# Chunk loop of a state-space scan with its outputs made with features on partitions, and a last norm in another order, on one Trainium2 core

## The reference, cut to what matters

```python
cs = jnp.cumsum(da, axis=2)                      # da = dt * a, per token and head
lmat = jnp.exp(jnp.where(tril, seg, -jnp.inf))   # seg = cs[t] - cs[s]
cb = jnp.einsum('bctgn,bcsgn->bctsg', cc, bc)
y_diag = jnp.einsum('bctsg,bctsgr,bcsgrp->bctgrp', cb, lmat, xs)        # xs = x * dt
chunk_states = jnp.einsum('bctgn,bctgr,bctgrp->bcgrpn', bc, decay_to_end, xs)
y_off = jnp.einsum('bctgn,bcgrpn,bctgr->bctgrp', cc, h_prev, jnp.exp(cs))
y = (y_diag + y_off)
...
y = y + d_skip[:, None] * xh
...
x = rmsnorm(x, norm_final)
```

## Time and profile before

| | |
|---|---|
| median of 3 runs | 1798.56 us (1798.55 to 1800.17) |
| the profiled execution | 1797.06 us, of which the span from the first to the last instruction is 1795.3 us |
| TensorE busy (PE) | 1782.7 us, 99% of the span |
| VectorE (DVE), ScalarE (ACT), GpSimd (POOL) | 935.5, 637.8, 831.1 us |
| mean granted clock of TensorE | 0.996 |
| chunk loop | from 206.2 to about 293 us |
| last norm and stores | from about 1780.9 us to the end |

### The profile page before, as it was taken

The page is one execution under the profiler, slowest core; times in us unless marked ns, Lnnn a source line. Parts: engine busy times, 40 slices in busy tenths (PEclk is TensorE's granted clock), DMA queues, the critical chain, the costliest instruction groups (busy, mean ns, idle before and its releaser), DMA issues.

```text
span 1795.3 us, 34076 instructions
## 1 busy us (share of the span) xinstructions
PE 1782.7 (99%) x13933; PEld 1741.7 (97%) x13933; DVE 935.5 (52%) x1507; ACT 637.8 (36%) x986; POOL 831.1 (46%) x410
## 2 busy tenths in 40 slices
PE   9999999999999999999999999999999999999998
PEld 8999899999999999999999999999999999999997
DVE  6577785666515524556444441554655425515465
ACT  6436464443212312344433331333433212312343
POOL 4333313675544544566433333333465535444563
PEclk9999999999999999999999999999999999999999
DMA  6222231223232232232222222122222222222231
GB/s 239 81 87 73 94 110 68 82 83 111 102 130 93 83 101 86 68 112 83 86 80 80 68 75 91 71 80 80 69 83 94 82 94 82 98 90 85 62 102 51
DMA packets 59684, 161.04 MB, mean 90 GB/s; under 512 B 6960, under 2 KB 21296, under 8 KB 59584
## 3 DMA queue, kind: packets, MB, share of 16 engines
q1 hardware_dynamic: 53088, 151.03, 24.3%
q10 hardware_dynamic: 6496, 8.61, 1.5%
HBM read 153.94 MB, written 5.67 MB: 89 GB/s over the span
## 4 chain that ended last, share of the span: by engine, by line
PE 97%; DVE 1%; DMA 0%; ACT 0%; POOL 0%; issue 0%; ACTq 0%; DVEq 0%; POOLq 0%
PE proj L321 86%; PE Q L1063 6%; PE proj L1063 2%; DMA x<-in_x 0%; PE Q L1295 0%; PE Q L1373 0%; DVE arena L1969 0%; PE Q L1247 0%; PE Q L1329 0%; POOL arena L671 0%; DVE rstd L372 0%; PE Q L1321 0%; PE Q L1090 0%; PE Q L1330 0%; PE Q L333 0%
## 5 line engine op out<-in xcount | busy, mean ns | idle before, releaser
L417 POOL TENSOR_TENSOR w_lo<-w_raw,w_hi 128x1024 fp32r<-128x1024 f32 (+2 forms) x275 | 659.1, 2397 | 753.7 <-ACT w_hi L343 743.5
L321 PE MATMUL proj<-op_hi,w_hi 128*128 128x256 f32 x4208 | 880.1, 290 | 1.0 <-DVE op_lo L1564 0.4
L321 PE MATMUL proj<-op_hi,w_lo 128*128 128x256 f32 x4208 | 870.1, 288 | 0.0
L321 PE MATMUL proj<-op_lo,w_hi 128*128 128x256 f32 x4208 | 863.0, 286 | 0.0
L321 PEld LDWEIGHTS proj<-op_hi,w_hi 128*128 128x128 f32 x4208 | 672.7, 188 | 14.7 <-issue 11.4
L321 PEld LDWEIGHTS proj<-op_lo,w_hi 128*128 128x128 f32 x4208 | 675.2, 188 | 0.0
L321 PEld LDWEIGHTS proj<-op_hi,w_lo 128*128 128x128 f32 x4208 | 671.2, 188 | 0.0
L343 ACT ACTIVATE w_hi<-w_raw 128x1024 fp32r<-128x1024 f32 (+2 forms) x275 | 283.7, 1031 | 657.7 <-PE proj L321 652.6
L1634 DVE TENSOR_TENSOR arena<-proj,rstd 128x512 f32<-128x512 f32 x141 | 97.4, 691 | 209.0 <-PE proj L321 200.9
L1641 DVE TENSOR_TENSOR x<-proj,x 128x512 f32<-128x512 f32 x72 | 49.7, 690 | 240.9 <-PE proj L321 240.9
L678 ACT ACTIVATE arena<-arena 128x128 f32<-128x128 f32 (+6 forms) x298 | 129.1, 474 | 57.8 <-DVE arena L1637 29.8
(11 more groups left out here) (198 smaller groups left out, 1004.5 us busy)
## 6 DMA issues: line engine op xcount, KB each, us to landing
w_raw<-in_w_gu SPq DMA_DIRECT2D x88, 512.0 KB, 3.3
w_raw<-in_w_down SPq DMA_DIRECT2D x32, 512.0 KB, 3.2
w_raw<-in_w_heads_a SPq DMA_DIRECT2D x30, 512.0 KB, 3.3
w_raw<-in_w_heads_b SPq DMA_DIRECT2D x18, 512.0 KB, 3.2
w_raw<-in_w_gate SPq DMA_DIRECT2D x16, 512.0 KB, 3.3
w_raw<-in_w_xbc SPq DMA_DIRECT2D x12, 512.0 KB, 3.3
w_raw<-in_w_down SPq DMA_DIRECT2D x16, 384.0 KB, 2.9
w_raw<-in_w_u SPq DMA_DIRECT2D x8, 512.0 KB, 3.3
```

Source lines behind the costliest of these rows:

```text
L321: last = nc.tensor.matmul(proj[:, 2 * g.mod(2) + half, 0:size], w[:, lo:lo + P], o[:, at:at + size], start=(k == 0 and j == 0), stop=(k == ...
L417: nc.gpsimd.tensor_tensor(w_lo[:, c:c + width], w_raw[:, c:c + width], w_hi[:, c:c + width], ALU.subtract).then_inc(w_lo_done, 1)
```

## The change: what it does

The y turn is gone. `diagonal` takes `xs` as the stationary side (64 columns wide) and 128 columns of `mix` as the moving one, and writes even heads to partitions 0 to 63 and odd heads to 64 to 127 of PSUM. `from_state` takes four tiles of the state as stationary and C as moving, four products of 128 columns where there was one of 512. The outputs then stand with features on partitions. exp(cs) must now lie along the free axis: ScalarE makes it on the turned `cs_t`, it goes to DRAM (`ecs_rows`), and SyncE fetches it for each chunk but chunk 1 into `y_run`, spread over the partitions (`decays_in`, two DMAs). `off_scaled` waits for it. `xs` is made by VectorE straight from PSUM in two halves, so ScalarE's two copies of x are gone. At the end one `keep_warm` is gone, `spread(0)` comes after all sums, and the store of tile 3 moves from SyncE's queue to ScalarE's, ahead of the stores of tiles 0 to 2.

```diff
+            def decays_in(p):
+                c, rows = (NC, TS) if p == 0 else (p - 1, CH)
+                if p:
+                    sp.wait_ge(sem("y_stored"), 2 * p)
+                else:
+                    sp.wait_ge(sem("ecs_kept"), 16)
+                    sp.wait_ge(sem("x_silu"), XBC)
+                for odd in range(2):
+                    dst = y_run[odd * SP_:(odd + 1) * SP_, :].rearrange("p (f t) -> p f t", f=KD)[:, :, 0:rows]
+                    src = ecs_rows.rearrange("(f two) t -> two f t", two=2)[odd, :, c * CH:c * CH + rows]
+                    sp.dma_start(dst, src.unsqueeze(0).broadcast_to([SP_, KD, rows])).then_inc(sem("decays_in"), 16)
+
             for b in range(4):
                 rows_in(0, b)
             weights("outa")
             weights("z", only=0)
+            decays_in(0)
             for p in range(NC + 1):
                 if p < NC:
                     for b in range(4):
                         rows_in(p + 1, b)
                 for n in SSD_MIXED[p] + SSD_END[p]:
                     weights("z", only=n)
+                if FRESH <= p < NC:
+                    decays_in(p + 1)
...
                 for half in range(2):
                     if p:
-                        pe.wait_ge(sem("y_stored"), 2 * p - 1 + half)
+                        if p == FRESH + 1:
+                            pe.wait_ge(sem("y_stored"), 2 * p - 1 + half)
+                        else:
+                            pe.wait_ge(sem("y_sum"), (2 * p - 2 if p <= FRESH else 2 * p - 4) + half + 1)
...
                 def from_state(g):
-                    mm(Q[0:rows, 2 + g, :], cols(10 + g), state[:, g * 512:(g + 1) * 512]).then_inc(sem("y_off"), 1)
+                    for f in range(4):
+                        last = mm(Q[:, 2 + g, f * P:f * P + rows], state[:, (4 * g + f) * P:(4 * g + f + 1) * P], cols(10 + g))
+                    last.then_inc(sem("y_off"), 1)
...
                     for j in range(4):
                         h = 4 * b + j
-                        last = mm(Q[0:rows, b // 2, (h % 8) * SP_:(h % 8 + 1) * SP_],
-                                  mix[0:rows, b * 512 + j * P:b * 512 + j * P + rows], xs[0:rows, h * SP_:(h + 1) * SP_])
+                        odd, at = h % 2 * SP_, h % 8 // 2 * P
+                        last = mm(Q[odd:odd + SP_, b // 2, at:at + rows], xs[0:rows, h * SP_:(h + 1) * SP_],
+                                  mix[0:rows, b * 512 + j * P:b * 512 + j * P + rows])
...
-                for half in range(2):
-                    pe.wait_ge(sem("y_sum"), 2 * p + half + 1)
-                    for f in range(4):
-                        last = nc.tensor.transpose(Q[:, half, f * P:f * P + rows],
...
-                    last.then_inc(sem("y_turned"), 1)
...
-                    dve.wait_ge(sem("xs_done"), p + 1)
-                    tt(heads3(x_tok[:, g * 512:(g + 1) * 512]), Q[0:rows, 2 + g, :].rearrange("p (h q) -> p h q", q=SP_),
-                       per_head(ecs, 8 * g, 8, rows), mul).then_inc(sem("y_scaled"), 1)
+                    dve.wait_ge(sem("decays_in"), 32 * (p + 1 if p < FRESH else p))
+                    y = four(y_run[:, g * 512:(g + 1) * 512])[:, :, 0:rows]
+                    tt(y, four(Q[:, 2 + g, :])[:, :, 0:rows], y, mul).then_inc(sem("y_scaled"), 1)
...
                 token_sums(half, chunks, ssq, 0)
-                if half:
-                    keep_warm()
-                    spread(0, HALVES[0][2])
                 pe.wait_ge(sem("last_sq"), half + 1)
...
-            spread(1, HALVES[1][2])
+            for half, (at, size, chunks) in enumerate(HALVES):
+                spread(half, chunks)
```

More of the change, by code:

```diff
@@ L219, in build @@
         r = Region(temps)
-        x_tok, xs, xsd, mix = (r.take(n) for n in (D, D, D, 4 * 512))
+        y_run, xs, xsd, mix = (r.take(n) for n in (D, D, D, 4 * 512))
         z_buf = arena[:, temps:temps + 2 * T]
         s_prompt, s_sample = r.take(D), r.take(D)
-        (dt_b, da, cs, ecs, dte, etot, p_d) = (r.take(NP_) for _ in range(7))
+        (dt_b, da, cs, dte, etot, p_d) = (r.take(NP_) for _ in range(6))
         cs_t = v_sq[0:SH, 0:T]
+        ecs_t = v_sq[0:SH, VT:VT + T]
         cs_rows = nc.dram_tensor("cs_rows", (SH, T), F, kind="Internal").ap()
+        ecs_rows = nc.dram_tensor("ecs_rows", (SH, T), F, kind="Internal").ap()
         ms_v = ssq[:, 0:(NC + 1) * GROUPS]
@@ L567, in _ @@
             for half, (lo, size, chunks) in enumerate(HALVES):
-                for k in range(Y_POOL, KD):
+                for k in range(Y_POOL + 1, KD):
                     sp.wait_ge(sem("y_out"), half * (KD - Y_POOL) + k - Y_POOL + 1)
@@ L774, in _ @@
                     act.wait_ge(sem("cs_copied"), 1)
-                    run(ecs, cs, ACT.Exp)
+                    act.wait_ge(sem("cs_turned"), 2)
+                    run(ecs_t, cs_t, ACT.Exp, "ecs_turned")
+                    act.wait_ge(sem("ecs_turned"), 1)
+                    act.dma_start(ecs_rows, ecs_t).then_inc(sem("ecs_kept"), 16)
                     run(dte, dte, ACT.Exp)
@@ L1053, in _ @@
             for half, (lo, size, chunks) in enumerate(HALVES):
-                for k in range(Y_POOL):
-                    act.wait_ge(sem("y_pool"), half * Y_POOL + k + 1)
+                for k in (Y_POOL, *range(Y_POOL)):
+                    if k == Y_POOL:
+                        act.wait_ge(sem("y_out"), half * (KD - Y_POOL) + 1)
+                    else:
+                        act.wait_ge(sem("y_pool"), half * Y_POOL + k + 1)
                     act.dma_start(part(O["y"], k, lo, size), part(p_proj, k, lo, size)).then_inc(stored, 16)
@@ L1844, in chunk @@
                     .broadcast_to([rows, nh, SP_])
-                dve.wait_ge(sem("x_copied"), 3 * p + 2)
                 if p:
                     dve.wait_ge(sem("y_mm"), 4 * p)
-                tt(heads3(xs), heads3(x_tok), per_head(dt_b, 0, SH, rows), mul).then_inc(sem("xs_done"), 1)
-                dve.wait_ge(sem("x_copied"), 3 * p + 3)
+                for half in range(2):
+                    dve.wait_ge(sem("x_turned"), 3 * p + half + 1)
+                    tt(heads3(xs[:, half * 512:(half + 1) * 512]), heads3(Q[:, half, :]), per_head(dt_b, 8 * half, 8, rows),
+                       mul).then_inc(sem("xs_done"), 1)
+                dve.wait_ge(sem("x_copied"), p + 1)
                 cb = two(bc_tok[0:rows, 256:512])[:, :, 0:rows]
@@ L1881, in chunk @@
                     add_to_x(group("outa", n), At(n))
-                if p == FRESH:
-                    dve.wait_ge(sem("xs_done"), p + 1)
-                else:
+                if p != FRESH:
                     dve.wait_ge(sem("y_scaled"), offs + 2)
-                for g in range(2):
+                for g in () if p == FRESH else range(2):
                     dve.wait_ge(sem("y_mm"), 4 * p + 2 * g + 2)
-                    y = x_tok[0:rows, g * 512:(g + 1) * 512]
-                    if p == FRESH:
-                        nc.vector.tensor_copy(y, Q[0:rows, g, :]).then_inc(sem("y_sum"), 1)
-                    else:
-                        tt(y, Q[0:rows, g, :], y, add).then_inc(sem("y_sum"), 1)
+                    y = four(y_run[:, g * 512:(g + 1) * 512])[:, :, 0:rows]
+                    tt(y, four(Q[:, g, :])[:, :, 0:rows], y, add).then_inc(sem("y_sum"), 1)
                 for g in () if p == FRESH else (1, 0):
```

23 lines of the change are left out of this document (10 added, 13 removed).

## The result

The changed kernel takes 1807.66 us (median of 6 runs, 1806.19 to 1808.9) where the kernel before, run beside it, takes 1798.47 us (6 runs, 1796.92 to 1800.17). The ratio is 1.005, 95% interval [1.0039, 1.006]: 9.2 us slower, outside my range of 1794.4 to 1804.0. Its profiled execution took 1808.0 us, span 1805.9 us at a mean clock of 0.991; before it was 1795.3 us at 0.996.

What follows compares the result with a forecast made beforehand. TensorE, 97% of what ended last, was taken as the bound. Terms -3.5 + 0.4 + 0.2 + 3.0 + 1.5 - 0.4 = +1.2 us on 1798.56 gave 1799.7 us, range 1794.4 to 1804.0.

Steps and rivals of the forecast that it cites:

- The diagonals: Diagonal products of chunks 1 to 4: unchanged at 112 ns an instruction, plus 0.1 us per chunk for changing form, +0.4 us.
- halves side by side: Rival: even and odd heads' diagonals run at once in different array columns, -5.7 us, -3.1 net, 1796.6 us; chance 0.30.
- The decays of chunks 2 to 4: Decay loads behind z loads on SyncE's queue: chunk 3's third group of diagonals waits +1.5 us, chunks 2 and 4 none.
- if z's data must pass first: Upper bound for chunk 3's wait on its decay loads: +2.4 us instead of +1.5.
- In time: Decay loads of chunks 2 and 4 cause no wait; chunk 2 ready at 247.1 against 248.0 due, chunk 4 alike.
- The decays of chunk 0: Chunk 0's loads behind z slab 0 make the third group of diagonals 3.1 us late, then half clock: +3.0 us.
- The y turn: Removing this TensorE piece from chunks 1 to 4 saves 0.88 us each, with nothing in its place: -3.5 us.
- `from_state`, the copies of x and the two halves on VectorE: Four state products instead of one: +0.2 us at most; VectorE and ScalarE changes have slack and count nothing.
- The last norm: At the kernel's end, sums come earlier and the stores' stream starts 0.2 to 0.6 us earlier: -0.4 us.
- No gain from the form: Rival: load and stream add up to 160 ns per diagonal instruction, +6.1 us, 1805.8 us; chance 0.05.
- Half clock longer: Rival: half clock after chunk 0's wait holds through the first 8 us of chunk 1, +4 us, 1803.7 us; chance 0.16.
- Decays in time: Rival: decay loads of chunks 0 and 3 land early enough, leaving -4.2 us, 1794.4 us; chance 0.13.

Runs made afterwards that it cites:

- ahead: Changed kernel with all decay loads fetched into two alternating buffers and issued ahead of the z loads they stood behind; 1789.3 us, ratio 0.995.
- loads_first: Changed kernel, one buffer as before, with only each pair of decay loads issued ahead of the z load it stood behind; 1791.71 us, ratio 0.9959.
- filled: Changed kernel plus 31 unread TensorE products ahead of the third group of diagonals, loads left where they were; 1799.68 us, ratio 1.001.
- tail_only: Kernel before the change with only the new order at its end; 1797.33 us, ratio 0.9992.
- ahead_old_tail: The kernel of ahead, but with the end of the kernel before the change; 1789.12 us, ratio 0.9953.
- first_only: Changed kernel with only chunk 0's two decay loads moved ahead of the load of z slab 0; 1803.27 us, ratio 1.0033.
- apart: The kernel of ahead with heads reordered so that two or four in a row use the same half of the columns; 1790.29 us, ratio 0.9955.

## Why the prediction was wrong, point by point

**The diagonals.** I kept them at 112 ns with bounds of 67 and 160; they take 62.5, just below the lower one. The rival of halves side by side held, -6.3 us for four chunks where it said -5.7. By the Trainium skill (TensorE: Matmul & The Clock Gate, Part 3: Packing small matmuls) products at different column positions run at once; the traces agree, with 104 against 62.5 ns, 1.7 times as fast for two halves. Having no row for the form, I chose the row that it was nearest to in columns. That step was wrong in size, but to the other side: by this alone the kernel would have been faster. The 0.1 us per chunk for going to the new form was right: the pair ahead of the diagonals starts 0.34 us before them (258.25 and 258.59 in `ahead`), where it was 0.25 (263.65 and 263.90).

**"The decays of chunks 2 to 4" is the step that failed**, in four of its terms.

The landing. I gave the loads 3.9 us from the row of the four `rows_in`. They took longer (issues between 260 and 275: operation, KB each, median us from issue to landing):

```profile
arena<-ecs_rows SPq DMA_DIRECT2D x2, 256.0 KB, 5.2
```

The load of z with its 512 KB goes out 0.39 us ahead of them on the same queue, itself held back by GpSimd's split. In chunk 2 that split ended later than I assumed: z went out 1.5 us after the chunk's start, where the earlier trace rows had 0.5. The chain of chunk 3 (start, length, what):

```profile
261.57 2.37 POOL w_lo L419
...
263.96 0.34 SPq L483
...
264.35 0.59 SPq L545
...
264.98 5.55 DMA arena<-ecs_rows
...
272.56 1.98 PE Q L1081 x16
```

From the first issue to the last landing that is 264.35 to 270.53, 6.2 us, where my sum had 4.3 (261.0 to 265.3). I had named this case ("if z's data must pass first") and gave it 0.9 us more; it was 1.9. `loads_first` shows how much of that is z. There the pair of chunk 3 goes out with z 3.7 us behind it, and lands 4.4 us after each issue; the changed kernel's took 4.9 and 5.6. So some 0.5 us against my 3.9 are the loads' own, which a row of `rows_in` did not tell, 0.5 to 1.2 us come with z ahead, and 0.2 is the second issue, later than I had it. But z need not be ahead: in chunk 2 of `loads_first` it goes out 1.8 us behind the pair, whose second load then takes 5.7 us, from first issue to last landing 6.3. The two rows, of chunk 3 and of the chain of chunk 2:

```profile
arena<-ecs_rows SPq DMA_DIRECT2D x2, 256.0 KB, 4.4
...
237.03 5.70 DMA arena<-ecs_rows
```

What these loads suffer from is z's data moving at the same time, by this reading, and not only its place in the queue. No run put them on another queue.

The due time. With cheaper diagonals the third group is due earlier in its chunk, so the same late load costs more: 7.5 us after the start in chunks 2 and 3, where it was 8.0. The rival of halves side by side counted this for itself, the sum did not. For chunk 3 these two terms are the miss: 1.5 us forecast, 1.9 for the landing and 0.5 for the due time make 3.9 of the 4.05 measured.

Chunks 2 and 4. "In time" was wrong: 2.44 and 3.10 us. In chunk 2, 0.9 us of slack were used up by the late z load (0.9 us), the landing (6.0 us from first issue to last landing, not 4.3) and the due time. Chunk 4 is not like chunk 2. Its loads wait for the z load and then for `y_stored`, and VectorE was late itself: its last operations of chunk 3, which end in `y_stored`, take 4.34 us, where those of chunk 2 take 2.17, and end at 284.81 (a split of GpSimd ran beside them, from 281.75 to 284.13); the loads go out at 284.83, 0.3 us after the issue of z. I said the wait for `y_stored` "adds nothing", which held only for a VectorE that is on time.

```profile
280.47 4.34 DVE L1926 SCALAR_TENSOR_TENSOR arena<-arena,vec 128x128 f32<-128x128 f32 x8
...
290.98 1.29 DVE L1885 TENSOR_TENSOR arena<-Q,arena 128x512 f32<-128x512 f32 x2 [2.55 <-DMA arena<-ecs_rows]
```

The clock. I charged a lower clock in chunk 0 alone, where the trace of before had it. With the waits of 4.05 and 3.10 us it fell in chunks 3 and 4 as well, for 6.8 and 3.4 us. I priced a wait at its length and not at what comes after it. `filled` shows what all half clock is worth, that of chunk 0 included: 7 to 8 of the 9 us.

By the terms of the sum: for chunks 2 to 4 I had 1.5 us, and measured are 9.6 us of waits and 4.2 to 4.7 of half clock behind them. That is some 12.5 us too little. The diagonals were 6.3 us too dear, chunk 0 was 1.4 us too cheap, and chunk 1 had a wait of 0.6 that I left out. Together this is 8 us, the distance from 1799.7 to 1807.7. So the number is too low by the difference of two large errors.

**The decays of chunk 0.** The mechanism was right and so was the wait: loads out at 212.00 (I said 212.1), VectorE free of its wait at 216.45 (215.8, at most 216.4), and the third group started at 217.18, 3.7 us after the earlier trace rows where I said 3.1.

```profile
216.45 0.49 DVE L1885 TENSOR_TENSOR arena<-Q,arena 128x128 f32<-128x128 f32 x2 [7.47 <-DMA arena<-ecs_rows]
```

Mis-sized was the half clock: I had it from about 216.4 to 225, it was 213.7 to 227.3. `to_state` took 3.71 us from start to start instead of my 3.4, and the chunk was 4.4 us longer than before, not 3.0.

**The y turn.** Right: chunk 1, where no decay load is waited for, is 1.5 us shorter: 0.9 for the turn and 1.6 for the diagonals, less a wait of 0.59 us and the rest. **`from_state`, the copies of x and the two halves on VectorE** had room, as I said, but mostly because TensorE waited elsewhere. Where no load is late, TensorE does wait for VectorE: 0.59 us in chunk 1 of the changed kernel, 1.10 and 0.95 us in chunks 1 and 2 of `ahead`.

**The last norm.** -0.8 us in the one profile against my -0.4, but `tail_only` and `ahead_old_tail` show that neither can be told from the scatter of single traces.

**The rivals.** "No gain from the form" came nearest in time (1805.8), and that is luck: it had the diagonals at 160 ns, and they take 62.5. "Half clock longer" (1803.7) had the right kind of cost in the wrong place: I put it into chunk 1 behind chunk 0; it came in chunks 3 and 4, each with its own wait. "Decays in time" I priced at 1794.4; `ahead` is that case together with the halves side by side, and takes 1789.3. I gave the two together no more than the low end of a range.

## What to carry to other kernels

When a DMA is added, look in the queue at what the issue ahead of it waits for and which large loads will be in flight beside it, and ask what else is queued behind the instruction that will wait. Price a wait of some 2 to 5 us on TensorE with the half clock that may follow it (here 7 to 8 us beside waits of 14.9). Where the wait can't be removed, unread products in it can be worth more than they cost. And when a step makes the waiting engine faster, move every due time with it before calling anything "in time".

## What was unexpected of the hardware

Two or four heads in a row in one half of the columns, followed by as many in the other, still take 2.08 us for 32 instructions, 68 ns each with the 0.11 us behind them, though with each half alone they take 104. If a product could only overlap its direct neighbour, `apart` should have been near 3 us by my estimate. How long a row in one half may be stays open: no run had one between four and eight heads.

A wait does not always bring the clock down. The 2.44 us in chunk 2 of the changed kernel left it at 1.00 for the whole chunk; 2.46 us in the same place in `first_only` was followed by half clock from 247.8 to 251.3. These runs don't tell what makes the difference.
